# A two-layer transformer trunk on one core: the last steps of each dense block token tile by token tile, and the norm inverse with its mean taken beside the root

## The reference

```python
def rms_norm(x, g):
    xf = x.astype(jnp.float32)
    y = xf * lax.rsqrt(jnp.mean(xf * xf, axis=-1, keepdims=True) + NORM_EPS)
    return (y * g.astype(jnp.float32)).astype(x.dtype)

def swiglu(h, w_gate, w_up, w_down):
    return (jax.nn.silu(h @ w_gate) * (h @ w_up)) @ w_down
...
        h = h + rms_norm(m, ln_mix_post[i])
        u = rms_norm(h, ln_ffn_pre[i])
        h = h + rms_norm(swiglu(u, ffn_w_gate[i], ffn_w_up[i], ffn_w_down[i]), ln_ffn_post[i])
```

## Time and profile before

| what | us |
|---|---|
| median of 3 runs | 769.05 |
| the profiled execution | 769.73 |
| its span, first to last instruction | 768.0 |
| last step of layer 0's dense block and boundary, from the first product of its first tile to the first product of the latent attention | 381.9 to 410.8 |
| last step of layer 1's dense block | 735.7 to 758.9 |
| from there to the end | 758.9 to 768.0 |

### The profile page before, as it was taken

The page is one execution under the profiler, slowest core; times in us unless marked ns, Lnnn a source line. Parts: engine busy times, 40 slices in busy tenths (PEclk is TensorE's granted clock), DMA queues, the critical chain, the costliest instruction groups (busy, mean ns, idle before and its releaser), DMA issues.

```text
span 768.0 us, 9977 instructions
## 1 busy us (share of the span) xinstructions
PE 709.0 (92%) x3601; PEld 592.0 (77%) x3601; DVE 425.6 (55%) x887; ACT 387.5 (50%) x726; POOL 15.9 (2%) x39
## 2 busy tenths in 40 slices
PE   3999999899989999999997898998998999999995
PEld 2789877777868888888875697887776888888883
DVE  4567456577765444555456464535675554444554
ACT  6455365676653344443353456667636433334442
POOL 7000000000000000000000000000000000000000
PEclk9997999999999999999998979999899999999998
DMA  9662323113347544456551323343333555544421
GB/s 316 222 204 71 110 55 122 45 56 110 111 139 241 195 164 164 166 193 214 204 206 35 90 87 92 108 147 110 111 109 111 186 211 206 206 174 164 164 110 55
DMA packets 55921, 111.02 MB, mean 145 GB/s; under 512 B 4224, under 2 KB 15536, under 8 KB 55888
## 3 DMA queue, kind: packets, MB, share of 16 engines
q1 hardware_dynamic: 54544, 106.24, 41.3%
q0 software_dynamic: 1344, 4.35, 1.6%
HBM read 109.54 MB, written 1.05 MB: 144 GB/s over the span
## 4 chain that ended last, share of the span: by engine, by line
PE 78%; ACT 9%; DVE 8%; issue 3%; DMA 2%; SPq 0%; DVEq 0%; ACTq 0%
PE bank L283 23%; PE bank L284 22%; PE bank L285 22%; DVE w_lo L275 3%; ACT w_hi L267 3%; PE bank L842 2%; PE bank L862 2%; ACT s_sb L1324 1%; PE bank L759 1%; DMA raw<-in_nsa_w_in 1%; PE bank L909 1%; PE bank L872 1%; DMA raw<-in_mla_w_in 1%; PE bank L957 1%; PE bank L495 1%
## 5 line engine op out<-in xcount | busy, mean ns | idle before, releaser
L275 DVE TENSOR_TENSOR w_lo<-raw,w_hi 128x2048 fp32r<-128x2048 f32 (+6 forms) x112 | 209.4, 1886 | 83.8 <-ACT w_hi L267 83.6
L283 PE MATMUL bank<-w_hi,act_lo 128*128 128x512 f32 (+3 forms) x528 | 208.4, 395 | 13.9 <-DVE w_lo L275 9.5
L285 PE MATMUL bank<-w_hi,act_hi 128*128 128x512 f32 (+3 forms) x528 | 199.0, 377 | 0.0
L284 PE MATMUL bank<-w_lo,act_hi 128*128 128x512 f32 (+3 forms) x528 | 198.8, 377 | 0.0
L267 ACT ACTIVATE w_hi<-raw 128x2048 fp32r<-128x2048 f32 (+6 forms) x112 | 175.2, 1585 | 12.1 <-PE bank L285 10.3
L283 PEld LDWEIGHTS bank<-w_hi,act_lo 128*128 128x128 f32 x528 | 103.5, 196 | 35.5 <-issue 8.6
L284 PEld LDWEIGHTS bank<-w_lo,act_hi 128*128 128x128 f32 x528 | 103.7, 196 | 18.0 <-issue 1.9
L285 PEld LDWEIGHTS bank<-w_hi,act_hi 128*128 128x128 f32 x528 | 103.2, 195 | 17.9
L1268 ACT ACTIVATE hidT_hi<-bank 128x512 fp32r<-128x512 f32 x20 | 12.0, 598 | 168.1 <-PE bank L759 168.1
L1664 DVE TENSOR_TENSOR hidT_lo<-bank,hidT_hi 128x512 fp32r<-128x512 f32 x20 | 13.8, 692 | 134.2 <-ACT hidT_hi L1268 134.2
L284 PE MATMUL bank<-w_lo,hidT_hi 128*128 128x512 f32 x160 | 63.0, 394 | 0.0
(11 more groups left out here) (212 smaller groups left out, 904.1 us busy)
## 6 DMA issues: line engine op xcount, KB each, us to landing
raw<-in_w_gate_up SPq DMA_DIRECT2D x44, 1024.0 KB, 5.3
raw<-in_w_down SPq DMA_DIRECT2D x22, 1024.0 KB, 5.0
raw<-in_nsa_w_in SPq DMA_DIRECT2D x6, 1024.0 KB, 9.7
raw<-in_w_q_up SPq DMA_DIRECT2D x8, 576.0 KB, 4.3
raw<-in_nsa_w_out SPq DMA_DIRECT2D x4, 1024.0 KB, 5.0
raw<-in_mla_w_in SPq DMA_DIRECT2D x4, 1024.0 KB, 6.2
raw<-in_mla_w_out SPq DMA_DIRECT2D x4, 1024.0 KB, 5.4
gain<-in_gains POOLq DMA_DIRECT2D x7, 512.0 KB, 5.8
```

The source lines that it names most:

```text
L275: ins = dve.tensor_tensor(lo[:, cols], raw[s][:, cols], hi[:, cols].bitcast(F32), ALU.subtract)
L283: pe.matmul(dst, a_lo, b_hi, start=start, stop=False)
L284: pe.matmul(dst, a_hi, b_lo, start=False, stop=False)
L285: return pe.matmul(dst, a_hi, b_hi, start=False, stop=stop)
```

## The change

Four things are changed.

1. **Last steps of both dense blocks.** PE does tile n - 1 for t = 0, the transposes of the step before, tile n for t = 0, and only then tile n - 1 for t = 1. The last hidden part is turned token tile by token tile (`turn_last`): two transposes for t = 0 before tile n for t = 1, two for t = 1 after down tile n + 1 for t = 0. ACT and DVE make silu, product and the split of the turned part for t = 0 alone and later for t = 1 (`last_hi`, `last_lo`, `hidden(j, ts)`), with the split of the last down tile between them.
2. **Last down products half by half.** `last_down` does the three plus three matmuls of half 0 and signals `half_done`, then half 1. For the dense blocks ACT squares half 0 at `half_done` and half 1 at the end, and DVE multiplies each half with the gain after ACT has squared it, for both token tiles.
3. **Norm inverses.** `root` signals when the bias is written and again when the root is. `invert` waits for the first signal, makes the mean and its product with -0.5, waits for the second, takes the reciprocal, and has two operations left. There are five operations as before. Inverses of the latent norms are called without the early wait.
4. **Before the last norm** ACT loads the root's table (`warm_root`) ahead of `post_root`.

```diff
+            dense = s % 2 == 1
+            if t == 0 and not dense:
                 act.wait_ge(sem("acc_done"), s + 1)
             for half in range(2):
-                if t == 0:
+                if dense:
+                    if half == 0:
+                        act.wait_ge(sem(f"half_done{s}"), t + 1)
+                    elif t == 0:
+                        act.wait_ge(sem("acc_done"), s + 1)
+                    else:
+                        wait_used(act, n)
+                elif t == 0:
...
         def gained(dve, s, t, n, halves=None):
-            if t == 0:
-                dve.wait_ge(sem("acc_done"), s + 1)
...
+            for half in halves or ((1, 0) if t == 0 and not dense else (0, 1)):
+                if dense:
+                    dve.wait_ge(sem(f"half_squared{s}"), 2 * t + half + 1)
...
+        def invert(tally, root_, total, width, rest, ready=None, at_=0, done=None):
             dve = tally.eng
             mean, b = newton[:, 0:1], newton[:, 1:2]
-            dve.reciprocal(root_, root_).then_inc(sem("inverted"), 1)
-            inverted[0] += 1
+            if ready is not None:
+                dve.wait_ge(ready, at_ - 1)
             tally.link(dve.tensor_scalar(mean, total, 1.0 / width, rest, ALU.mult, ALU.add))
-            dve.wait_ge(sem("inverted"), inverted[0])
+            tally.link(dve.tensor_scalar(mean, mean, -0.5, None, ALU.mult))
+            if ready is not None:
+                dve.wait_ge(ready, at_)
+            tally.link(dve.reciprocal(root_, root_))
             tally.link(dve.scalar_tensor_tensor(b, root_, mean, root_, ALU.mult, ALU.mult))
-            tally.link(dve.tensor_scalar(b, b, -0.5, 1.5, ALU.mult, ALU.add))
-            ins = dve.tensor_tensor(root_, root_, b, ALU.mult)
+            ins = dve.scalar_tensor_tensor(root_, b, 1.5, root_, ALU.add, ALU.mult)
...
+                def turn_last(t):
+                    pe.wait_ge(sem(f"hidden_ready{s}"), (STEPS - 1) * T + t + 1)
+                    pe.wait_ge(sem(f"hiddenT_ready{s}"), STEPS - 1 + t)
+                    for c in range(2):
+                        last = pe.transpose(bank[2][:, c * SEQ + t * P:c * SEQ + (t + 1) * P],
+                                            hid[:, t, c * P:(c + 1) * P], ident[:])
+                    last.then_inc(sem(f"hidden_turned{s}"), 1)
+
+                def last_down(n, t):
+                    pe.wait_ge(sem(f"hiddenT_ready{s}"), STEPS + t)
+                    project_down(pe, n, last_hidT_hi, last_hidT_lo, t, stop=True, halves=[0]) \
+                        .then_inc(sem(f"half_done{s}"), 1)
+                    return project_down(pe, n, last_hidT_hi, last_hidT_lo, t, stop=True, halves=[1])
...
-                project(pe, n - 1, both, 4, 512, 0)
+                project(pe, n - 1, both, 4, 512, 0, ts=[0], done=False)
                 turn_hidden((STEPS - 1) * T)
                 take(pe, n)
                 project(pe, n, both, 4, 512, 4, ts=[0], done=False).then_inc(sem(f"last_gate{s}"), 1)
+                project(pe, n - 1, both, 4, 512, 0, ts=[1])
+                turn_last(0)
                 project(pe, n, both, 4, 512, 4, ts=[1])
                 take(pe, n + 1)
-                pe.wait_ge(sem(f"hiddenT_ready{s}"), STEPS - 1)
                 project_down(pe, n + 1, hidT_hi, hidT_lo, 0)
-                turn_hidden(STEPS * T)
-                project_down(pe, n + 1, hidT_hi, hidT_lo, 1, [0])
+                turn_last(1)
                 take(pe, n + 2)
-                pe.wait_ge(sem(f"hiddenT_ready{s}"), STEPS)
-                project_down(pe, n + 2, last_hidT_hi, last_hidT_lo, 0, stop=True).then_inc(sem("acc_done"), 1)
-                project_down(pe, n + 1, hidT_hi, hidT_lo, 1, [1]).then_inc(weights_used, 1)
-                project_down(pe, n + 2, last_hidT_hi, last_hidT_lo, 1, stop=True).then_inc(weights_used, 1)
+                last_down(n + 2, 0).then_inc(sem("acc_done"), 1)
+                project_down(pe, n + 1, hidT_hi, hidT_lo, 1).then_inc(weights_used, 1)
+                last_down(n + 2, 1).then_inc(weights_used, 1)
...
-                split_hi(act, n + 2, SLOT)
                 act.wait_ge(sem(f"last_gate{s}"), 1)
                 silu_of(0)
+                split_hi(act, n + 2, SLOT)
+                last_hi(0)
                 wait_used(act, n)
                 silu_of(1)
                 if s == 1:
                     split_hi(act, MLA_IN, SLOT)
-                hidden_hi(STEPS - 1, last_hidT_hi)
+                last_hi(1)
...
+            warm_root(act)
             for t in range(T):
                 post_root(chain, 3, t, TILES - 1)
...
+                hidden(STEPS - 1, [0])
                 split_lo(dve, n + 2, SLOT)
-                hidden(STEPS - 1)
+                last_lo(0)
+                hidden(STEPS - 1, [1])
                 if s == 1:
                     split_lo(dve, MLA_IN, SLOT)
-                hidden_lo(STEPS - 1, last_hidT_hi, last_hidT_lo)
+                last_lo(1)
```

51 lines of the change are left out of this document (31 added, 20 removed).

## The result

The changed kernel takes 764.88 us (median of 19 executions, 760.00 to 768.08). The kernel before, timed beside it, takes 771.98 us (19 executions, 765.25 to 777.74), 2.9 us more than the median of the three runs shown before. The ratio is 0.9916, with a 95% interval of 0.9892 to 0.994: faster, as forecast, but the time lies 0.6 us outside the predicted range.

A forecast was written before the change was run, and what follows sets the result against it. PE was busy 92% of the span, so only stretches where the chain passes through ACT and DVE could shrink. 2.8 + 2.65 + 2.2 = 7.65 us off the profiled 769.73 gave 762.1, hence a median of 761.4, range 759.7 to 764.3.

The forecast's parts named there:

- The end of layer 1: From PE's last product to the last addition to h: 2.5 us against 5.2, a gain of 2.8 with PE's wait.
- The boundary after layer 0: Earlier load and split of the second MLA_IN tile bring h and the first latent-attention product 2.65 us earlier.
- The slack in the last step: At the transposes for t = 0, the product is ready 0.4 us before PE wants it, so nothing is late.
- late feeding: Rival: slack missing or load no quicker, PE stands 0.5 to 1.5 us per layer; 764 to 766.5; 0.10 with half effect.
- a slower kernel: Rival: the last down tile, split later, becomes the bound, 5.5 us late in each layer; 771 us; chance 0.02.
- The clock: First latent-attention products after layer 0's dense block stay at full clock since PE's gap shrinks: 2.2 us, bounds 0 and 2.5.
- its first rival: The clock falls anyway: chains shorter, first latent-attention products still slow; 763.6 us, or down to 762.8; chance 0.30.
- The two "almost equal" gaps: PE gaps at 426.9 to 429.6 and before 229.7: products ran at 0.50 after the first, 1.00 after the other.
- The sum: Whole kernel: 2.8 for layer 1's end, 2.65 for the boundary, 2.2 for the clock, together 7.65 us.
- the base: Whole kernel: profiled execution 769.73 us, 0.68 above the median of 769.05, so the median should go to 761.4.
- Part 3 elsewhere: Ten other norm inverses: mixers' ends gain 0.3 us each, four latent ones lose 0.1 each; taken as 0, 0.4 either way.

The follow-up runs named there:

- h1: The changed kernel with the norm inverses put back to the old order, reciprocal first and mean behind it; 766.34 us, one execution.
- f1: The kernel before with products of a zero tile in PE's waits at block and sub-layer boundaries and in latent attention; 766.31 us, ratio 0.9915.
- h2: The changed kernel without the early load of the root's table at the end of layer 1; 766.83 us, one execution.
- e3: The kernel before with only the new norm inverses, mean and its factor ahead of the root; 771.27 us, ratio 0.9981.
- f3: The kernel before with zero products only around the transposes of h at the end of layer 0; 767.52 us, ratio 0.994.
- e2: The kernel before with only the last down products, squares and gains half by half, plus the early table load; 765.27 us, ratio 0.9905.
- e1: The kernel before with only the last dense steps done token tile by token tile; 764.76 us, ratio 0.9914.
- g3: The changed kernel with late second MLA_IN split and zero products, fewer at layer 0's end, six among the narrow products; 760.47 us, ratio 0.9822 without the slowest execution.
- f2: The changed kernel with zero products in PE's waits at the boundaries and in latent attention; 760.12 us, ratio 0.984 to the kernel before.
- g1: The changed kernel with the second MLA_IN tile split later, behind token tile 0's root and additions; 762.04 us, ratio 0.987 to the kernel before.
- g2: The changed kernel with the second MLA_IN tile split late and zero products in PE's waits; 760.28 us, ratio 0.9848 to the kernel before.

## Why the prediction was right and where it went wrong

**The end of layer 1: right.** 2.49 us from PE's end to the last h against 2.5 forecast, 3.04 in the stretch against 2.8, the rest being PE 0.33 earlier. The reason given for part 3 (DVE is at the gain until after the root is there) is what the rows of the changed kernel and h1 show.

**The boundary after layer 0: right, for a load as in the profile before.** The changed trace reaches the mark 1.74 us earlier than before, for reasons ahead of it; put on the old time scale, the high part starts at 396.80 (forecast 396.9), h at 403.23 (403.35), the first product at 408.00 (408.15). 2.81 us against 2.65. The prediction took the load's 6.28 us as given; with the quicker load that f1 shows the gain would be 1.95.

**The slack in the last step: right.** PE has no idle time at the new transposes. This is the place that the prediction called the tightest, in the timelines of DVE and PE of the changed kernel:

```profile
737.20 0.48 DVE L1695 SCALAR_TENSOR_TENSOR pT<-bank,stats,pT 128x256 f32<-128x256 f32 x1
```
```profile
737.86 0.38 PE L793 MATMUL bank<-ident,pT 128*128 128x128 f32 x2
```

0.2 us to spare, where 0.4 was forecast. The rivals of late feeding and of a slower kernel fall with it.

**The clock: the right size in the profile, the wrong kind of number.** The profiled execution gave the 2.2 us. But h1 and h2, whose PE waits at this place are those of the changed kernel, lost 1.55 of them. The forecast and its first rival were written as two worlds, with 0.55 and 0.30; in fact both outcomes occur with the same code up to this place. The Trainium skill (TensorE: Matmul & The Clock Gate, Part 1) says that the number of slow matmuls of one kernel differs from run to run, and the traces agree: 5.70 us in two executions of the changed kernel, 7.25 in h1 and h2. The two "almost equal" gaps of the prediction have the kernel's own four zero products ahead of one of them (226.44 us), not of the other; but in the changed kernel the gap behind these four is followed by half the clock as well, so these products don't decide.

**The step that failed: the base and its scatter.** The sum, 7.65 us, was near: the medians differ by 7.10 us, the means of all executions with a recorded clock (56 of before, 26 of the changed kernel) by 8.1. That it was so near is in part luck: the two chains were worth 5.85, and the rest goes with a clock whose slow stretches lie all over the kernel, not only where the sum priced one. What failed is "it lay 0.68 above the median of 769.05, so the median should go to 761.4". Three runs within 0.2% of one another were taken for what the kernel does. 19 executions have a median of 771.98, and of the 72 executions of before other than those three only 12 took 769.40 us or less. Three such in a row would be rare by chance; the clock of the three wasn't recorded, and why they were fast stays open. With the base of 771.98 the same sum gives 764.3, against 764.88 measured. And the range took in the one slow stretch at this boundary and, at its low end, one more, 2.2 us each, where a kernel that meets a handful of such stretches scatters over 8 us (760.00 to 768.08): a median of the changed kernel could not be known to better than this from three runs of before. Read in windows of 4 us, the granted clock is below 1.00 in these stretches (the end, where PE has finished, left out): before, 56 to 68, 88 to 92, 124 to 132, 408 to 416, 428 to 436, 444 to 460 and 536 to 548 us; after, 60 to 64, 224 to 232, 436 to 448, 468 to 476, 528 to 540 and 572 to 580. The first three of before and the first two of after lie far ahead of the last steps.

How much of the gain is the clock? Over some 150 timed executions of all kernels, within one kernel 0.001 of mean granted clock goes with 0.51 us. The mean clock is 0.967 before and 0.974 after: 3.6 us. At an equal clock (0.98) the kernels stand so, with standard errors of 0.2 to 0.5 us:

| before | e3 | f3 | f1 | e2 | e1 | changed | g3 | f2 | g1 | g2 |
|---|---|---|---|---|---|---|---|---|---|---|
| 765.7 | 765.8 | 765.3 | 763.3 | 762.8 | 761.9 | 761.1 | 760.1 | 759.8 | 759.3 | 758.4 |

e1 is 3.8 us from before (its stretches 3.78), e2 2.9 (3.71), the changed kernel 4.6 (5.85), f3 not distinguishable. The reckoning is rough, since it takes the clock's idle stretches with the busy ones: f1 stands 2.4 us below before, where its two stretches are 0.86 us shorter. But it sets e1 and e2 between before and the changed kernel, as their traces do and the medians don't. By it and by the stretches shorter chains gave 4.6 to 5.9 us, fewer slow products the rest. Why the mean clock itself is higher in the changed kernel is only partly shown: f3 says that with hardly any wait at this one boundary it is 0.975 in place of 0.967.

**Part 3 elsewhere: not measured by itself.** The prediction took nothing, with 0.4 us either way. e3's total, 0.2% lower with an interval from 0.5% lower to 0.1% higher, can't tell that.

## What to carry to other kernels

Find what the change touches in the trace, put a mark ahead of it and one behind, and measure between them: here such a stretch repeats within 0.05 us where whole executions scatter by 8, unless a load stands in it. Before you forecast a time, ask how many executions stand behind the base, and widen the range by the number of stretches in which the clock may fall, not by the one that you looked at. An operation that is moved beside a wait pays only as long as that wait is there; a second edit that removes the wait takes the gain of the first with it.

## What the runs showed of the hardware

- PE's granted clock after a wait is not settled by the code: with the same waits of 0.73 and 1.20 us in front, the same 24 products took 5.70 us in two executions (clock 1.00) and 7.25 in those of h1 and h2 (0.76). h1 and h2 ran on another chip than the second of the two.
- Extra matmuls on zeros in PE's waits made a kernel faster by 6.4 us (f1), and at one boundary alone by 5.0 (f3), both of medians.
- One load of 1 MB in the same place of the program doesn't always take the same time: ACT waited 0.56, 1.77 and 2.02 us for it (f1, before, f3).
- The clock also falls where PE is never idle: in 436 to 446 us of g2 and g3 it is 0.50, with PE busy for 10.00 us of 10.00. Six zero products of 512 columns among the narrow ones there did not prevent it (g3).
- The load of the root's table takes 1.28 us on ACT. At the end of layer 1 it costs nothing in either place (28.15 and 28.16 us to the last h), since both ACT and DVE wait for PE there.
